# Preparing the second half's first chunk inside the first half's final residual

## The reference: what is computed

```
h   = rms_norm(x, norm_w) * (1 + scale) + shift     # scale, shift, gate: from c @ ada_w + ada_b
mix = mixer(h)                                       # its input projection, the mixer
x   = x + gate * (mix @ w_out)                       # residual
```

## Time and profile before

| | us |
|---|---|
| median of 3 runs | 3396.36 (3396.12 to 3396.7) |
| the profiled execution | 3398.87 |
| its span in the trace | 3397.1 |
| mean granted TensorE clock | 0.988 of full |
| TensorE / VectorE / ScalarE / GpSimd busy | 97% / 69% / 45% / 28% of the span |

### The profile page before, as it was taken

The page is one execution under the profiler, slowest core; times in us unless marked ns, Lnnn a source line. Parts: engine busy times, 40 slices in busy tenths (PEclk is TensorE's granted clock), DMA queues, the critical chain, the costliest instruction groups (busy, mean ns, idle before and its releaser), DMA issues.

```text
span 3397.1 us, 49814 instructions
## 1 busy us (share of the span) xinstructions
PE 3288.2 (97%) x19249; PEld 2643.3 (78%) x19249; DVE 2338.7 (69%) x3628; ACT 1528.0 (45%) x2757; POOL 962.3 (28%) x495
## 2 busy tenths in 40 slices
PE   7999999999999999999989999999999999999998
PEld 4777787777988778788867777877779777778877
DVE  6887789766668866656567777896536664666555
ACT  5666575333344124333466755753334431343334
POOL 1005343211143124232610052432111522332253
PEclk9999999998999999999989999999999999999999
DMA  6432355456843613211241133554449221231113
GB/s 204 120 111 83 85 161 143 121 162 196 316 152 103 193 59 94 56 38 32 82 145 42 49 88 89 158 136 131 125 123 359 83 57 45 68 83 43 38 52 104
DMA packets 573144, 384.78 MB, mean 113 GB/s; under 512 B 72186, under 2 KB 526573, under 8 KB 572909
## 3 DMA queue, kind: packets, MB, share of 16 engines
q1 hardware_dynamic: 572909, 381.60, 37.5%
HBM read 299.93 MB, written 80.54 MB: 112 GB/s over the span
## 4 chain that ended last, share of the span: by engine, by line
PE 73%; DVE 14%; ACT 4%; DMA 3%; issue 2%; SPq 2%; POOL 2%; PEldq 0%; ACTq 0%; DVEq 0%; PEld 0%; POOLq 0%
PE bank L236 57%; DVE dnp_conv L2060 3%; PE bank L255 2%; DVE dnp_diag_inv L2134 2%; PE bank L2608 1%; DVE h_lo L793 1%; DVE dnp_diag_term L2131 1%; DMA dn_planes<-dnp_inv_t 1%; POOL w_lo L218 1%; PE bank L2878 1%; PE bank L2864 1%; DVE res_h L781 1%; DVE pool_ada_sums L302 1%; PE bank L2362 1%; PE bank L2353 1%
## 5 line engine op out<-in xcount | busy, mean ns | idle before, releaser
L236 PE MATMUL bank<-h_hi,w_hi 128*128 128x512 f32 x3520 | 1427.1, 405 | 21.8 <-DVE h_lo L793 8.0
L236 PE MATMUL bank<-h_hi,w_lo 128*128 128x512 f32 x3520 | 1378.5, 392 | 0.0
L236 PE MATMUL bank<-h_lo,w_hi 128*128 128x512 f32 x3520 | 1378.4, 392 | 0.0
L218 POOL TENSOR_TENSOR w_lo<-w_raw,w_hi 128x1024 fp32r<-128x1024 f32 x262 | 649.2, 2479 | 1291.5 <-ACT w_hi L209 1290.7
L236 PEld LDWEIGHTS bank<-h_hi,w_hi 128*128 128x128 f32 x3520 | 664.6, 189 | 196.8 <-issue 31.2
L236 PEld LDWEIGHTS bank<-h_hi,w_lo 128*128 128x128 f32 x3520 | 664.2, 189 | 143.7
L236 PEld LDWEIGHTS bank<-h_lo,w_hi 128*128 128x128 f32 x3520 | 665.2, 189 | 141.7 <-issue 12.7
L209 ACT ACTIVATE w_hi<-w_raw 128x1024 fp32r<-128x1024 f32 x292 | 307.8, 1054 | 324.4 <-PE bank L236 222.3
L2060 DVE SCALAR_TENSOR_TENSOR dnp_conv<-dnp_raw,dn_conv_w,dnp_conv 128x512 f32<-128x512 f32 x288 | 268.7, 933 | 177.2 <-ACT dnp_conv L1865 170.0
L127 POOL TENSOR_TENSOR h_lo<-y,h_hi 128x512 fp32r<-128x512 f32 x72 | 112.9, 1581 | 497.9 <-ACT h_hi L118 497.4
L873 DVE SCALAR_TENSOR_TENSOR x_res<-bank,mod_gate,x_res 128x512 f32<-128x512 f32 x128 | 95.7, 748 | 125.2 <-PE bank L236 95.6
(11 more groups left out here) (358 smaller groups left out, 4602.2 us busy)
## 6 DMA issues: line engine op xcount, KB each, us to landing
dnr_in<-dn_planes SPq DMA_DIRECT2D x112, 512.0 KB, 7.2
dn_planes<-y SPq DMA_DIRECT2D x192, 256.0 KB, 2.8
w_raw<-in_dn_w_in SPq DMA_DIRECT2D x64, 512.0 KB, 4.6
y<-in_ada_w SPq DMA_DIRECT2D x80, 256.0 KB, 4.6
w_raw<-in_swa_w_in SPq DMA_DIRECT2D x36, 512.0 KB, 3.7
w_raw<-in_rg_w_in SPq DMA_DIRECT2D x32, 512.0 KB, 4.7
w_raw<-in_rg_w_out SPq DMA_DIRECT2D x32, 512.0 KB, 4.0
w_raw<-in_dn_w_out SPq DMA_DIRECT2D x32, 512.0 KB, 4.0
```

What stands on the lines that cost most here:

```text
L218: alu.tensor_tensor(self.lo[j % SLOTS][:, :, :], self.raw[j % 2][:, :, :], self.hi[j % SLOTS][:, :, :].bitcast(F32), ALU.subtract).then_in ...
L236: ins = self.nc.tensor.matmul(out, w[slot][:, k, :], x[:, k, cols], start=(k == 0 and n == 0), stop=(k == KT - 1 and n == 2))
```

## The change

What the ingest of half 1 did for chunk 0 moves into the final residual of half 0 (`nxt`), and the ingest of half 1 (`early`) keeps the turning and normalising of chunk 1.

- SyncE: the eight row loads of x are issued at steps 8 (rows 0 to 3, after a wait for the last `h_lo`), 9 (4, 5) and 10 (6, 7), each behind that step's weight load.
- PE: in steps 11 to 14 it turns two tiles of the next chunk 0 per step into bank 6, one before the product and one behind it. The factor matmuls (`sum_next`) stand ahead of product 13 and behind product 15. The final sum of chunk 1 waits for both factors to be copied (`s_r`), since bank and buffers are shared.
- ScalarE: it squares row tiles 0 to 3 in step 10, 4 and 5 in step 12, 6 and 7 in step 13; it copies the even tiles behind the rounding of steps 11 to 14; the first factor in step 12, the second behind the last rounding; its part of norms 0 to 7 in steps 13 (0), 14 (1, 2), 15 (3, 4) and behind (5 to 7).
- VectorE: it copies the odd tiles in steps 11 to 14, makes the diagonals in steps 11 and 14, and does its passes of the norms at the same places. The intermediate `hf` is now two PSUM banks (7, 5) in place of four SBUF buffers.
- Ingest of half 1: eight turns (chunk 1), copied alternately by ScalarE and VectorE, which need wait only for PE to have left the phase before. Both wait for all engines before the norms. Chunk 1's factor lies in `y[:, 0, cs[0]]`, written by ScalarE at the end of the phase before.
- Half 0's ingest and half 1's final residual are as before.

```diff
+NEXT_FROM, NEXT_SUMS = KT + 3, (5, 6)
+NEXT_ROWS = {KT: (0, 1, 2, 3), KT + 1: (4, 5), KT + 2: (6, 7)}
+NEXT_SQUARES = {KT + 2: (0, 1, 2, 3), KT + 4: (4, 5), KT + 5: (6, 7)}
+NEXT_NORMS, NEXT_LATE = {KT + 5: (0,), KT + 6: (1, 2), KT + 7: (3, 4)}, 5
...
+    nxt, early = final and half + 1 < core.halves, ingest and half > 0
+    steps = [(c, d) for c in range(1 if early else 0, NCH) for d in range(KT)]
...
+        if nxt:
+            rstd = total[0][:, :]
+            hf = [core.bank[i][:, :] for i in (7, 5)]
...
             for j in range(0 if ingest else len(steps)):
                 w.load_to(sp, min(tile0 + j + 4, after))
+                if nxt and j == KT:
+                    for i in range(2):
+                        sp.wait_ge(core.y_split[i], (core.y_base + len(steps)) // 2)
+                if nxt:
+                    load_x(core, A, sp, half + 1, NEXT_ROWS.get(j, ()))
                 if final and j == KT + 5:
                     store_rows(0)
...
+            def turn_next(d):
+                if d:
+                    pe.wait_ge((s_nx, s_nd)[(d - 1) % 2], (d - 1) // 2 + 1)
+                else:
+                    pe.wait_ge(core.x_loaded[0], 16 * 4 * (half + 2))
+                for t in range(ROWS):
+                    ins = nc.tensor.transpose(core.bank[SPARE][:, t * P:t * P + P], y[:, t, d * P:d * P + P],
+                                              core.ident[:, :])
+                ins.then_inc(s_nt, 1)
+
+            def sum_next(c):
+                pe.wait_ge(s_diag, c + 1)
+                if c:
+                    pe.wait_ge(s_nx, KT // 2)
+                    pe.wait_ge(s_nd, KT // 2)
+                else:
+                    pe.wait_ge(s_rms, 1)
+                spread(core.bank[sums[c]], s_ns)
...
                 pe.wait_ge(s_add, KT * c + KT)
+                if nxt and c:
+                    pe.wait_ge(s_r, NCH)
...
+                if nxt and j == NEXT_FROM + 2:
+                    sum_next(0)
+                if nxt and 0 <= j - NEXT_FROM < KT // 2:
+                    turn_next(2 * (j - NEXT_FROM))
...
@@ PE, behind product j and the output turn @@
+                if nxt and 0 <= j - NEXT_FROM < KT // 2:
+                    turn_next(2 * (j - NEXT_FROM) + 1)
+                if nxt and j == len(steps) - 1:
+                    sum_next(1)
...
@@ VectorE, behind take_rows and scale_rows of step j @@
+                    if nxt and j == NEXT_FROM:
+                        spread_rows(0)
+                    if nxt and 0 <= j - NEXT_FROM < KT // 2:
+                        m = j - NEXT_FROM
+                        dve.wait_ge(s_nt, 2 * m + 2)
+                        nc.vector.tensor_copy(x[:, 2 * m + 1, cs[0]], core.bank[SPARE][:, :]).then_inc(s_nd, 1)
+                    if nxt and j == len(steps) - 2:
+                        spread_rows(1)
+                    if nxt:
+                        for k in NEXT_NORMS.get(j, ()):
+                            norm_dve(dve, 0, k)
...
@@ ScalarE, behind the rounding of step j @@
+                if nxt and 0 <= j - NEXT_FROM < KT // 2:
+                    act.wait_ge(s_nt, 2 * (j - NEXT_FROM) + 1)
+                    act.wait_ge(s_tout, KT)
+                    nc.scalar.activation(x[:, 2 * (j - NEXT_FROM), cs[0]], core.bank[SPARE][:, :], ACT.Copy).then_inc(s_nx, 1)
...
@@ ScalarE, at the end of step j @@
+                    if nxt:
+                        if j == NEXT_FROM + 1:
+                            take_factor(0)
+                        for r in NEXT_SQUARES.get(j, ()):
+                            if r % ROWS == 0:
+                                act.wait_ge(core.x_loaded[r // ROWS], 16 * 4 * (half + 2))
+                            square_row(*divmod(r, ROWS))
+                            if r % ROWS == ROWS - 1:
+                                root_rows(r // ROWS)
+                        for k in NEXT_NORMS.get(j, ()):
+                            norm_act(act, 0, k)
...
@@ ScalarE, behind step 15 @@
             w.round_to(act, after)
+            if ada or nxt:
                 take_factor(1)
+            for k in range(NEXT_LATE, KT if nxt else 0):
+                norm_act(act, 0, k)
```

More of the change, by code:

```diff
@@ L358, in stack_rows, with load_x @@
     return rows
-def load_x(core, A, sp, half):
-    for t in range(HALF // P):
+def load_x(core, A, sp, half, rows=range(HALF // P)):
+    for t in rows:
         at = half * HALF + t * P
@@ L564, in residual_phase @@
     h_hi, h_lo, x, y = core.h_hi, core.h_lo, core.x, core.y
-    banks = ring_banks(layer, NCH * KT)
+    nxt, early = final and half + 1 < core.halves, ingest and half > 0
+    cs = [slice(c * CH, c * CH + CH) for c in range(NCH)]
+    steps = [(c, d) for c in range(1 if early else 0, NCH) for d in range(KT)]
+    sums = NEXT_SUMS if nxt else SUMS
+    banks = ring_banks(layer, len(steps))
     before = last_users(banks)
@@ L573, in residual_phase @@
     with ExitStack() as ctx:
-        if ingest:
-            squares = core.sb(f"{tag}_squares", [P, D], F32, ctx)
-            diag = core.sb(f"{tag}_diag", [P, ROWS, P], F32, ctx)
+        if ingest and not early:
+            squares = core.sb(f"{tag}_squares", [P, D], F32, ctx)[:, :].rearrange("p (t k) -> p t k", t=ROWS)
+            diag = core.sb(f"{tag}_diag", [P, ROWS, P], F32, ctx)[:, :, :]
+        if nxt or ingest and not early:
             row_ssq, row_root, row_rstd = (core.sb(f"{tag}_row_{n}", [P, NCH, ROWS], F32, ctx) for n in ("ssq", "root", "rstd"))
@@ L585, in residual_phase @@
             total = [core.sb(f"{tag}_sq_total{i}", [P, CH], F32, ctx) for i in range(NCH)]
[L586 to L589, removed]
+        if nxt:
+            rstd = total[0][:, :]
+            hf = [core.bank[i][:, :] for i in (7, 5)]
+            s_nt = core.sem(f"{tag}_next_x_turned")
+            s_nx, s_nd = (core.sem(f"{tag}_next_x_copied_by_{e}") for e in ("act", "dve"))
+            s_ns = core.sem(f"{tag}_next_summed")
+        elif not final:
+            if not early:
+                rstd = core.sb(f"{tag}_rstd", [P, CH], F32, ctx)[:, :]
+                logv = core.sb(f"{tag}_log", [P, CH], F32, ctx)
+            hf = [core.sb(f"{tag}_h{i}", [P, CH], F32, ctx)[:, :] for i in range(NHF)]
         s_xt = core.sem(f"{tag}_x_transposed")
@@ L627, in residual_phase @@
         engines = ENGINES[:4] if ingest and half else ENGINES
+        norm_col = 0 if ingest or nxt else (layer + 1) * KT
+        norm0 = KT if early else 0
         def projected(j):
@@ L658, in _ @@
             w.load_to(sp, after)
[L659 to L662, removed]
             core.clear_last(sp)
@@ L673, in _, with spread @@
                 core.fence(pe)
+            def spread(out, done):
+                nc.tensor.matmul(out[:, :].rearrange("p (t k) -> p t k", t=ROWS), core.ones[:, :], diag,
+                                 start=True, stop=True).then_inc(done, 1)
+            def turn_next(d):
[15 more added lines that the diff above has]
+                spread(core.bank[sums[c]], s_ns)
             def sum_squares(c):
@@ L744, in _ @@
                                each_k=core.y_is_split(c) if d == 0 else None)
-                if d == 0 and c and not ada:
+                if d == 0 and c and not ingest:
                     sum_squares(c - 1)
@@ L762, in _ @@
                 sum_squares(NCH - 1)
-            else:
+            elif not early:
                 core.sum_last = lambda: sum_squares(NCH - 1)
-            if ada:
+            if ingest:
                 pe.wait_ge(s_x, len(steps) // 2)
@@ L976, in _ @@
                         .then_inc(s_x, 1)
+            if early:
+                core.fence(act, engines)
+            if ada:
                 for c in range(NCH):
@@ L981, in _ @@
                     root_rows(c)
-            for j, (c, d) in enumerate(() if ada else steps):
+            for j, (c, d) in enumerate(() if ingest else steps):
                 if not ingest:
```

99 lines of the change are left out of this document (44 added, 55 removed).

## The result

The changed kernel takes 3403.32 us (median of 17 runs, 3400.59 to 3410.39), the kernel before 3398.33 (17 runs, 3395.73 to 3403.11): ratio 1.0015, 95% interval 1.0008 to 1.0021. It is slower by some 5 us, less than the 6.8 us (0.2%) that the prediction took as telling from no change. The forecast of 3402.5 is 0.8 us away, and its case is the one that happened. The forecast difference is the fairer measure, since the kernel before has a median 2.0 higher here than the 3396.36 that the prediction started from: +6.1 was forecast, and the medians differ by 5.0.

A forecast was written before the change was run, and what follows sets the result against it. TensorE (PE), busy 97% of the span, was taken as the bound. The terms summed as +18.2 - 10.3 - 1.8 = +6.1 us, from 3396.36 to 3402.5, with a range of 3394 to 3412.

The forecast's parts named there:

- its case: Whole kernel: the prediction's own case, +2 to +10 us, given 60%, split 32 slower and 28 same.
- Term 1: Final residual, steps 11 to 14: grows by 14.5 us of work and standing plus 3.7 of clock, +18.2.
- Term 2: From product 15's end to the second half's first product: 20.0 us instead of 30.3, so -10.3.
- term 3: From the second half's first product to steady products: 21.8 us instead of 23.6, so -1.8, between -2.9 and 0.
- Step 12's stop of 0.15 for VectorE: Residual, step 12: PE stops 0.15 us for VectorE's copy, most of which the factor's matmul hides.
- half of one 3.35: Residual, the three steps after step 11: clock loss counted as 1.7 us, between 0 and 3 x 3.35.
- the first: Rival: the clock holds in the residual, 14.5 us instead of 18.2, total +2.4, 3398.8 us; 15%.
- the second: Rival: the clock falls in each of four steps, 13.4 us in place of 3.7, total +15.8, 3412 us; 13%.
- own bound for half clock, 21.5: Product 15 to the second half's first product: 21.5 us if the turns run at half clock.
- VectorE's row scaling and diagonal fit in before that: Residual, step 11: both fit in before VectorE's copy of tile 1, 0.69 us, for which PE stops 1.0 more.
- the 1.4 for a start at half clock: Second half's first products: 1.4 us added to three products of 16.4 for starting at half clock.
- The third rival: Residual: PE not stopped, only 4.4 us of work remain, total -7.7, 3388.7 us; 12%, shared with a tail of 14.

The follow-up runs named there:

- e2: Changed kernel with ScalarE's copy of the even tile ahead of its rounding; residual 7.5 us shorter, time 1.2 outside the expected 3396.5 to 3398.5.
- e3: Changed kernel with weight tile 18 rounded behind the residual's last row scaling, not ahead of the second factor; tail 0.35 us shorter.
- e6: e5 with weight tile 18 rounded, and its low part taken, behind the second half's evacuations of x; product 15 to first product 20.4 us instead of 22.6.
- e7: e5 with chunk 0's four row squares spread over steps 9 and 10, two each; 3396.29 us.
- e1: Changed kernel with two of four row squares moved from step 10's end to step 9's; PE stops 2.93 us for ScalarE's copy, 2.49 for VectorE's.
- e5: e2 with each step's even tile turned in the middle of the product, not ahead of it; residual 39.1 us.
- e10: e9 with three of the four row squares in step 9 and one in step 10; ratio 0.9969 to the kernel before.
- e11: e5 unchanged, run once more; 3397.03 us.
- e9: e8 with VectorE's copy of a turned tile ahead of its row scaling and diagonal in step 11; ratio 0.9973 to the kernel before.
- e8: e7 with weight tile 18 rounded behind the evacuations and one norm more inside the residual; time missed 3387 to 3390 us by 2.2.

## Why the prediction was right

The mechanism was right in terms 1 and 2, with sums 1.0 too favourable each, and one step of term 3 was wrong the other way. That the errors cancel to 0.6 in the trace is luck, and so is part of the 0.8 in time.

**Term 1, the residual: +18.2 predicted, +19.2 measured.** By steps, from one output turn to the next less the 5.93 of a step before (step 11 with the one new turn ahead of its product; products 12 and 14 took 7.01 and 7.11 instead of 5.50):

```
            predicted, without clock    measured    of it at half clock
step 11     6.5                         8.95        1.5 product 12, 1.0 turns
step 12     3.15                        3.4
step 13     3.15                        5.0         1.6 product 14
step 14     1.7                         1.9
sum         14.5                        19.2        4.1
```

The stops came where they were put: 3.94 (4.1 predicted) and 0.88 (1.0) in step 11, 1.25 once in each of steps 12 to 14, and 0.88 (1.0) in step 13. Together 9.45, 10.1 predicted. Step 12's stop of 0.15 for VectorE did not come. With 4.4 of work and 4.1 of clock this makes 18.0; the other 1.2 lies in hand-overs around the six waits (the time from one engine's end to the next one's start beyond the idle time shown), which the prediction took as nothing. The squares ran from 1698.20 to 1702.89 (1697.8 to 1702.8 predicted), and e2 shows the cause of the later stops: with the copy ahead of the rounding, every stop of 1.25 is gone.

The clock was costed at 3.7 and took 4.1. The fall behind the long stop was right, 2.0 predicted and 2.5 measured. For the other three steps half of one 3.35 was taken, as a weighing of chances; one of them did fall, for 1.6. That these two numbers agree is chance. Neither rival on the clock held: it did not stay (the first), and it did not fall four times (the second).

**Term 2, the tail: -10.3 predicted, -9.3 measured.** PE's last sum waits for the second factor as said, and norm 6's pass is shut out, 2.51. The scaling starts 12.6 after product 15 (13.1 predicted) and the first evacuation by ScalarE 15.06 (15.3). The mis-sized part is what follows: VectorE's last copy ends at 20.5 instead of 19.4, while PE turns the last five tiles at a granted clock of 0.58 (1758.5 to 1762.6), and the first product waits 1.25 for that copy. The sum had these turns at full clock; the prediction's own bound for half clock, 21.5, lies nearer to the 21.0 measured than its 20.0. As for the shut-out, e3 and e6 price it only together with the rounding: the scaling starts 1.75 earlier after product 15 without both, and in e6 that reaches the first product.

The Trainium skill (SBUF — State Buffer, "Who interferes with whom") has VectorE's 2-port modes contend with GpSimd, with `tensor_scalar` among the operations that can enter them, besides instructions with two SBUF inputs. The traces agree as far as they go: L894, a scaling with one tensor input that takes 0.75 alone, takes 2.89 beside w_lo in e7; that it ran in such a mode no trace shows. The prediction named the norms' pass and the diagonal as what can be held up, and not the row scaling. The kernel before already had one row scaling of 2.68 (columns as in the earlier trace rows; L838 there, L894 in e7):

```profile
L838 DVE TENSOR_SCALAR res_stage<-res_stage,res_row_scale x8: 740/751/2680, 1700.9 to 3390.3; 128x1024 f32<-128x1024 f32 x8
L894 DVE TENSOR_SCALAR res_stage<-res_stage,res_row_scale x8: 740/753/2890, 1704.1 to 3388.3; 128x1024 f32<-128x1024 f32 x8
```

The prediction's step "VectorE's row scaling and diagonal fit in before that" held because ScalarE's copy was late enough. e1 and e7 moved that copy forward; e1 hit the diagonal and e7 the row scaling.

**Term 3, behind it: -1.8 predicted, -3.2 measured.** The step that failed is the 1.4 for a start at half clock: in the changed kernel the clock is 1.00 from the first product on. It isn't wrong in general, as e5, e10 and e11 show, whose first product starts at half clock and whose stretch is 21.9, 21.7 and 21.9 instead of 20.3. By luck it paid back most of what terms 1 and 2 lost by being 1.0 too kind each.

**The third rival** (no stops, 3388.7) did not happen, but the gain it names can nearly be had: e9, in which PE stands 0.6, takes 9.2 less in the trace and 9.7 less in time than before, where the rival had -7.7. But e9 has the late tile 18 and the norm moved forward, which the rival did not; the kernel with neither and no stop was not run. An estimate for it, from e9's residual, e7's tail and the 20.3 behind it, is 5.5 - 8.5 - 3.2 = -6.2.

So the change moves 9.3 + 3.2 us of work out of the border and pays 19.2 for it, of which only 4.4 is the work. The other 14.8 are standing, hand-overs and clock. They come from the order in the queues of ScalarE and VectorE, which PE waits for, and from the place of the turns in PE's own: e9, which changes these three and spreads the squares, pays 1.1 of them.

## What to carry to other kernels

Work put into the gaps of a busy engine costs its own time only if what it waits for is done by then: where two uses of one bank follow each other, put something long between them, and give the copy that frees the bank the first place in its engine's queue, ahead of work that has slack. Taking away the longest wait alone brought nothing to the residual (e1, e7); list what is queued ahead of the next releaser, and what else in that queue can be stretched, before moving anything. A late piece of side work must be moved past everything on the path, not only past the instruction that it disturbed (e3 against e6).

## What the runs showed of the hardware

- Falls of TensorE's clock after short stops: a stop of 2.95 was followed by 1.6 us of loss in e5 and e11 and by none in e6; one of 2.12 by as much in e7, one of 2.07 by none in e8; stops of 1.25 and 0.88 in step 13 were followed by 3.3 us at half clock, while 1.25 in step 12 and 14 were not. The Trainium skill (TensorE: Matmul & The Clock Gate, "What's actually happening") says of a kernel's start that how many matmuls run before the clock rises varies from run to run of the same kernel. What these traces show, in mid-kernel, is variation between nearly identical kernels; the one that was repeated did the same twice.
- A scaling of 128x1024 by VectorE takes 0.75 alone and 2.89 beside GpSimd's w_lo (e7), the diagonal 0.69 and 2.76 (e1); VectorE's copies of 128x512 out of a bank stay at 0.68 to 0.69 around the border of the halves in every run.
- In front of the rms of step 10 ScalarE loads a function table, 1.28 us. It stands on the way to PE's stop in step 11 in the changed kernel as in e9, where ScalarE has no idle time from its rounding at 1696.99 to the copy at 1703.69. Moving it was not tried.
- With rows of x in the queue, the rounding of weight tile 12 starts 1.2 (e9) to 3.0 us (e1) later against product 10's end than before. The next tile is rounded late, too, only in e1 (1.5 after product 10) and e10 (1.7, in part for its third square).
